# The weighted sum of expert rows moves from VectorE to TensorE

## The reference, cut to what matters

```python
top_s, pos = lax.top_k(combo, PEER_TOPK)
expert = jnp.take_along_axis(ids, pos, axis=-1)
g = jax.nn.softmax(top_s, axis=-1).astype(hb.dtype)
u_sel = peer_u[expert]
a = jax.nn.gelu(jnp.einsum('bqhkd,bqd->bqhk', u_sel, hb))
v_sel = peer_v[expert]
return jnp.einsum('bqhk,bqhkd->bqd', g * a, v_sel)
```

## Time and profile before

| | |
|---|---|
| time, three runs | 2165.31, 2167.11, 2168.97 us; median 2167.11 |
| profiled execution, span | 2165.9 us |
| PE, DVE busy | 1586.9 us (73%), 1510.4 us (70%) |
| gathered rows | 256 x 1 MB = 268.45 MB, by POOL's queue |
| first gather issued, last one issued | 329.8, 1203.6 us |
| last row sum begins | 1233.1 us |

### The profile page before, as it was taken

The page is one execution under the profiler, slowest core; times in us unless marked ns, Lnnn a source line. Parts: engine busy times, 40 slices in busy tenths (PEclk is TensorE's granted clock), DMA queues, the critical chain, the costliest instruction groups (busy, mean ns, idle before and its releaser), DMA issues.

```text
span 2165.9 us, 24713 instructions
## 1 busy us (share of the span) xinstructions
PE 1586.9 (73%) x9616; PEld 1356.3 (63%) x9616; DVE 1510.4 (70%) x2224; ACT 584.5 (27%) x880; POOL 598.4 (28%) x376
## 2 busy tenths in 40 slices
PE   7999999930007999729400176688999999899997
PEld 2975779930006888614200046688898988598997
DVE  2673695799998778598799975867543744666554
ACT  3433420000002220010000134443443344244443
POOL 1542523243333343334344444533000000000000
PEclk9999995555557999959755598899999999999999
DMA  7444459997788999989999415354542554043442
GB/s 311 156 188 184 157 210 381 422 413 287 303 299 309 424 423 422 423 335 404 409 391 396 167 56 210 141 201 158 205 156 78 195 194 157 0 183 138 186 173 100
DMA packets 57567, 538.46 MB, mean 249 GB/s; under 512 B 6384, under 2 KB 6512, under 8 KB 7152
## 3 DMA queue, kind: packets, MB, share of 16 engines
q1 hardware_dynamic: 20592, 268.48, 31.6%
q0 software_dynamic: 36864, 268.45, 31.1%
HBM read 535.86 MB, written 1.05 MB: 248 GB/s over the span
## 4 chain that ended last, share of the span: by engine, by line
PE 48%; DVE 26%; issue 11%; DMA 11%; ACT 2%; POOL 1%; POOLq 0%; DVEq 0%; SPq 0%; ACTq 0%
PE psum L385 48%; DVE arena L1582 10%; DMA arena<-in_experts,idx_stage 9%; DVE ring_r L1224 3%; DMA ring<-in_w_ffn 1%; DVE small L1579 1%; DVE arena L1621 1%; DVE arena L1571 1%; DVE small L1571 1%; DVE rstd L1251 1%; DVE arena_r L1273 1%; DVE arena L1475 1%; DVE small L1473 1%; DVE small L1524 1%; ACT ring_r L904 0%
## 5 line engine op out<-in xcount | busy, mean ns | idle before, releaser
L1224 DVE TENSOR_TENSOR ring_r<-ring,ring_r 128x1024 fp32r<-128x1024 f32 (+1 forms) x240 | 348.8, 1463 | 284.3 <-ACT ring_r L904 283.1
L385 PE MATMUL psum<-small_r,ring_r 128*128 128x256 f32 x2304 | 438.5, 292 | 65.9 <-DVE ring_r L1224 55.7
L385 PEld LDWEIGHTS psum<-small_r,ring_r 128*128 128x128 f32 x2304 | 375.9, 199 | 70.7 <-DVE ring_r L1224 39.8
L853 POOL DMA_INDIRECT arena<-in_experts,idx_stage x256 | 299.7, 1171 | 389.0 <-DVE arena L1582 314.2
L1571 DVE CUSTOM_DVE_ANT_0 arena<-arena 128x1024 f32<-128x1024 f32 x256 | 313.5, 1225 | 105.9 <-DMA arena<-in_experts,idx_stage 97.0
L1582 DVE SCALAR_TENSOR_TENSOR arena<-arena,small 128x1024 f32<-128x1024 f32 x256 | 335.1, 1309 | 9.2
L385 PE MATMUL psum<-h_t_r,ring_r 128*128 128x256 f32 x1152 | 335.7, 291 | 0.0
L385 PE MATMUL psum<-arena_r,ring_r 128*128 128x256 f32 x2208 | 322.2, 280 | 3.0 <-DVE arena_r L1273 3.0
L904 ACT ACTIVATE ring_r<-ring 128x1024 fp32r<-128x1024 f32 (+1 forms) x240 | 247.9, 1041 | 279.3 <-PE psum L385 207.6
L385 PEld LDWEIGHTS psum<-arena_r,ring_r 128*128 128x128 f32 x2208 | 286.5, 190 | 3.5 <-DVE arena_r L1273 3.4
L1126 ACT ACTIVATE small<-small 128x2 f32<-128x2 f32 x128 | 26.0, 203 | 780.0 <-DVE small L1571 779.9
(11 more groups left out here) (222 smaller groups left out, 1843.3 us busy)
## 6 DMA issues: line engine op xcount, KB each, us to landing
ring<-in_w_ffn SPq DMA_DIRECT2D x33, 2048.0 KB, 11.8
ring<-in_w_in SPq DMA_DIRECT2D x31, 2048.0 KB, 10.2
ring<-in_w_ada SPq DMA_DIRECT2D x30, 2048.0 KB, 11.0
ring<-in_w_ffn SPq DMA_DIRECT2D x24, 1408.0 KB, 9.9
ring<-in_w_out SPq DMA_DIRECT2D x4, 2048.0 KB
ring<-in_peer_wq SPq DMA_DIRECT2D x4, 2048.0 KB, 7.8
ring<-in_p_ret SPq DMA_DIRECT2D x4, 2048.0 KB
arena<-in_experts,idx_stage POOLq DMA_INDIRECT x256, 9.5
```

Source lines behind the costliest of these rows:

```text
L385: return nc.tensor.matmul(o, a, b, start=first, stop=last)
L853: nc.gpsimd.indirect_dma_start(rows[slot % GBUF], None, dram["experts"], bass.IndirectOffsetOnAxis(ap=idx_stage[:, slot:slot + 1], axis=0) ...
L1224: nc.vector.tensor_tensor(whole(i, ring_r), whole(i, ring), upper(i).bitcast(F32), ALU.subtract).then_inc(lo_made, 1)
```

## The change

The weights and the additions move to PE. For every slot DVE writes a 128x128 diagonal matrix with gate x activation of each token on the diagonal (`diag_batch`, which takes the place of `sum_batch`). PE multiplies it with the `v` half of the row, in two float32 matmuls of 512 columns, and accumulates a token tile's 128 slots in PSUM banks 6 and 7. PE's second matmul increments `row_free`. At a tile's end ACT copies the two banks to `y_of[t]`. The work that PE had in one piece is cut into steps, and one step goes ahead of every second batch of diagonals; it has 6 banks in turn meanwhile. `diag` is a ring of 8.

```diff
-        weights = small[:, 1456:1472].rearrange("p (b n) -> p b n", b=8)
+        diag = small[:, 1536:2560].rearrange("p (b n) -> p b n", b=GBUF)
...
+            def background():
+                yield from modulation("ada2_", "w_ada_2", range(MOD_CTX), silu_c2, 2)
+                for _ in range(CHOICE_STEPS + 1 - MOD_CTX):
+                    yield
+                squares("ctx1", hid, KD)
+                pe.wait_ge(sem("h_ctx1"), 1)
+                yield from feed_forward("fc", 1, h_t)
+                yield
+                squares("ctx2", hid, KD)
+                pe.wait_ge(sem("h_ctx2"), 1)
+                yield from by_token("kc", "w_in_2", range(2, 4), h_t, "act")
+                yield from by_token("vc", "w_in_2", range(4, 8), h_t, "act")
+
+            cycle[:] = range(BANKS - 2)
+            bg = background()
+            for n in range(NT * SLOTS // BATCH):
+                if n % 2 == 0:
+                    next(bg, None)
+                t, first = divmod(n, SLOTS // BATCH)
+                if first == 0:
+                    for half in range(2):
+                        pe.wait_ge(*tenant[BANKS - 2 + half])
+                for g in range(n * BATCH, (n + 1) * BATCH):
+                    pe.wait_ge(sem("diag"), g + 1)
+                    for half in range(2):
+                        last = mm(psum[:, BANKS - 2 + half, :], diag[:, g % GBUF, :],
+                                  rows[g % GBUF][:, D + half * BANK:D + (half + 1) * BANK],
+                                  g % SLOTS == 0, g % SLOTS == SLOTS - 1)
+                    last.then_inc(sem("row_free"), 1)
...
             for t in range(NT):
-                pe.wait_ge(sem("experts"), t + 1)
+                pe.wait_ge(sem("y_out"), 2 * t + 2)
...
+                act.wait_ge(sem("row_free"), GBUF + SLOTS * (t + 1))
+                for half in range(2):
+                    nc.scalar.activation(y_of[t][:, half * BANK:(half + 1) * BANK], psum[:, BANKS - 2 + half, :],
+                                         ACT.Copy).then_inc(sem("y_out"), 1)
...
-            def sum_batch(n):
+            def diag_batch(n):
                 t, b = divmod(n, per_tile)
                 v.wait_ge(sem("gelus"), n + 1)
-                gate = flat(best[:, t])[:, b * BATCH:(b + 1) * BATCH]
-                step(TT(weights[:, n % 8, :], acts[:, n % 8, :], gate, ALU.mult))
                 for s in range(BATCH):
                     g = n * BATCH + s
-                    STT(y_of[t], rows[g % GBUF][:, D:2 * D], weights[:, n % 8, s:s + 1], y_of[t],
-                        ALU.mult, ALU.add).then_inc(sem("row_free"), 1)
-                    v.wait_ge(sem("row_free"), GBUF + g + 1)
+                    TS(diag[:, g % GBUF, :], ident, acts[:, n % 8, s:s + 1],
+                       flat(best[:, t])[:, b * BATCH + s:b * BATCH + s + 1], ALU.mult, ALU.mult).then_inc(sem("diag"), 1)
```

More of the change, by code:

```diff
@@ L332, in program @@
         row_landed = [sem(f"row_landed{i}") for i in range(GBUF)]
-        groups, index, turn = [], {}, {"act": 0, "dve": 0}
+        groups, index, bank_of = [], {}, {}
+        cycle, at_bank, tenant = list(range(BANKS)), [0], {}
         def phase_end(q):
@@ L356, in begin @@
             def begin(name, who):
-                i = len(groups)
-                if i >= BANKS:
-                    pe.wait_ge(drained[groups[i - BANKS][1]], groups[i - BANKS][2])
+                bank = cycle[at_bank[0] % len(cycle)]
+                at_bank[0] += 1
+                if bank in tenant:
+                    pe.wait_ge(*tenant[bank])
                 count = 1 + sum(g[1] == who for g in groups)
+                index[name] = len(groups)
+                bank_of[name] = bank
                 groups.append((name, who, count))
-                index[name] = i
-                return psum[:, i % BANKS, :]
+                tenant[bank] = (drained[who], count)
+                return psum[:, bank, :]
             def end(ins):
@@ L397, in by_token @@
                         end(last)
-                    release()
+                        if t == NT - 1:
+                            release()
+                        yield
             def squares(tag, sq, kb):
@@ L690, in _ @@
                 ada_turn(i)
[L693 to L700, removed]
+            def background():
+                yield from modulation("ada2_", "w_ada_2", range(MOD_CTX), silu_c2, 2)
+                for _ in range(CHOICE_STEPS + 1 - MOD_CTX):
+                    yield
+                squares("ctx1", hid, KD)
+                pe.wait_ge(sem("h_ctx1"), 1)
+                yield from feed_forward("fc", 1, h_t)
+                yield
+                squares("ctx2", hid, KD)
[18 more added lines that the diff above has]
+                    last.then_inc(sem("row_free"), 1)
+                if n % (SLOTS // BATCH) == SLOTS // BATCH - 1:
+                    for half in range(2):
+                        tenant[BANKS - 2 + half] = (sem("y_out"), 2 * t + half + 1)
+            for _ in bg:
+                pass
+            cycle[:] = range(BANKS)
             for t in range(NT):
-                pe.wait_ge(sem("experts"), t + 1)
+                pe.wait_ge(sem("y_out"), 2 * t + 2)
                 for i in range(2):
@@ L917, in take @@
                 act.wait_ge(group_done, index[name] + 1)
-                return psum[:, index[name] % BANKS, :]
+                return psum[:, bank_of[name], :]
             def drain(ins):
@@ L1162, in _ @@
                 act.wait_ge(group_done, index[f"mx{i}"] + 1)
-                nc.scalar.activation(flat(mixed_hi[:, 2 * i:2 * i + 2, :]), psum[:, index[f"mx{i}"] % BANKS, :],
+                nc.scalar.activation(flat(mixed_hi[:, 2 * i:2 * i + 2, :]), psum[:, bank_of[f"mx{i}"], :],
                                      ACT.Copy).then_inc(sem("mixed_hi"), 1)
@@ L1572, in dot_batch @@
                                                         dots[:, n % 8, s:s + 1]), sem("dots"))
-            def sum_batch(n):
+            def diag_batch(n):
                 t, b = divmod(n, per_tile)
                 v.wait_ge(sem("gelus"), n + 1)
-                gate = flat(best[:, t])[:, b * BATCH:(b + 1) * BATCH]
-                step(TT(weights[:, n % 8, :], acts[:, n % 8, :], gate, ALU.mult))
                 for s in range(BATCH):
                     g = n * BATCH + s
-                    STT(y_of[t], rows[g % GBUF][:, D:2 * D], weights[:, n % 8, s:s + 1], y_of[t],
-                        ALU.mult, ALU.add).then_inc(sem("row_free"), 1)
-                    v.wait_ge(sem("row_free"), GBUF + g + 1)
+                    TS(diag[:, g % GBUF, :], ident, acts[:, n % 8, s:s + 1],
+                       flat(best[:, t])[:, b * BATCH + s:b * BATCH + s + 1], ALU.mult, ALU.mult).then_inc(sem("diag"), 1)
             for t in range(NT):
                 gates(t)
-                step(nc.vector.memset(y_of[t], 0.0))
                 dot_batch(t * per_tile)
@@ L1593, in _ @@
                         dot_batch(n + 1)
-                    sum_batch(n)
+                    diag_batch(n)
                     if b % 2 == 1:
                         next(bg, None)
-                step(nc.vector.memset(stat[:, 0:1], 0.0), sem("experts"))
             for _ in bg:
```

## The result

The changed kernel takes 2300.94 us (median of 4, 2297.22 to 2302.66) against 2166.21 before: ratio 1.0623, 95% interval 1.0608 to 1.0638. The forecast was 2289, with a range of 2228 to 2372. The profiled execution has a span of 2300.8 us, 134.9 more than before. DVE begins to add the expert sums to x at 1366.9 us instead of 1234.5: 132.4 us of the difference lie in the expert layer, where the forecast had put 121.

What follows compares the result with a forecast made beforehand. Before, DMA bound A, C and E, and DVE B and F; after, PE mostly binds. Stretches sum to 1012 us against 891, +121, and +1 for end copies: 2288, median 2289 us, range 2228 to 2372.

Steps and rivals of the forecast that it cites:

- A: Layer stretch from 345 to 502 us before, the modulation; 10 periods of 19.8 us, 198 us forecast, +41.
- C: Layer stretch from 676 to 840 us before, 11 slabs of w13; 249 us forecast including a norm, +85.
- D: Layer stretch from 840 to 978 us before, 8 slabs of w2 and one empty period; 145 us forecast, +7.
- E: Layer stretch from 978 to 1125 us before, 12 steps of keys and values; 187 us forecast including a norm, +40.
- The rival of the collision: DVE's diagonal writes await POOL's gather issues, 4.8 us more per period in B: +56, 2345 us; chance 8 in 100.
- that of the low clock: PE's clock stays low in A and B, +78 and +44: 2411 us; chance 9 in 100.
- B: Layer stretch from 502 to 676 us before, no slab; 12 periods of 10.5 us, 126 us forecast, -48.
- That of the transfers: Transfers bind the layer and PE fits beneath: 785 us for the layer, so 2061 us; chance 4 in 100.
- F: Layer stretch from 1125 to 1236 us before, rows alone; 10 periods of 9.9 us plus 8, 107 us forecast, -4.
- The two norms: Norms of the context, priced in C and E: 17 us each, with 10 to 20 us as ends.
- The semaphore wait of each slot: Each slot's wait might expose a weight load of some 0.19 us: up to +32 us over 42 periods PE binds.
- The write: DVE's diagonal write of 128 columns, taken as 0.28 us, 72 us in all; ends 0.18 or 0.405 us.

Runs made afterwards that it cites:

- half of the matmuls: Changed kernel with the second of the two diagonal matmuls left out for all slots but a tile's first and last: 2186.41 us, ratio 1.0094.
- the tying alone: Kernel before, DVE's row sums kept, PE's list cut into one slab per 4 slots, then a wait for freed rows: 2170.73 us, ratio 1.0012.
- ACT's writes: Changed kernel, but ACT writes the diagonals and DVE only multiplies gate and activation: 2293.61 us, ratio 1.0593.
- mixed kernel: Changed kernel, but PE sums only batches 14 to 43 and 96 to 127, DVE the others; PE's slabs in one piece each: 2139.45 us, ratio 0.9861.
- POOL's wait: POOL's first late addition waits until all rows are freed: 2161.8 us in the kernel before; 2140.11 us when PE sums only batches 14-43 and 96-127.
- the later batch: PE sums batches 14-43 and the second tile from 101 instead of 96, DVE the others, POOL's late additions waiting: 2131.49 us, ratio 0.984.

## Why the prediction came out

**The direction and its cause were right.** The load on PE, 454 us by the sum of the rows, was 473 net (913 - 440). The diagonal matmuls alone make a group of 504 us, 440 at the price of full clock; the rest is their time at the low clock, and part of it is made up by the modulation, which ran partly at full clock. In A, C, D and E the time is a sum of PE's periods; with half of the matmuls 85% of the loss goes away, with the tying alone 4 us come. The rival of the collision is answered by the run with ACT's writes, that of the low clock by a clock of 0.70 in A and 0.88 in B. That of the transfers is answered by the run with half of the matmuls: it takes some 216 us (252 x 0.859) off PE, which leaves some 697 on PE, below the 785 us of that rival's sum, and still the kernel is at 2186 and not near 2061.

**By stretches**, forecast and measured: A 198 and 193; B 126 and 138.5; C 249 and 241.5; D 145 and 145; E 187 and 181.5; F 107 and 121.5. The sum was 1012 and came to 1021. That it is off by 9 only is partly luck: B and F were 27 us too short, A, C and E 18 too long.

- A: I had 9.4 us for 8 diagonals and 10.4 for the slab; it was 10.0 and 11.0, as the clock rose some 5.9 us into the diagonals (I took 4.5) and lasted 3 us into the slab (as taken). The stretch came out shorter all the same: its last two periods took 17.3 us, and the first of the ten slabs, which I had counted in, ran from 319.9 on, ahead of the rows and of the stretch. The 6 us until the first diagonals, at 351.2, go the other way.
- The price of a matmul was taken at 0.888 from keys and values, where some ran at the low clock. At full clock it is 0.859. With slabs of 13.8 and 6.87 us it makes a period of C 20.7 in place of 21.1 and one of E 13.7 in place of 14.2, 5 us in each stretch. The two norms, with the slower slab behind each, took 14 us in place of 17. In E the late cut hides 3 us.
- D met its 145 us by luck: its 8 periods with a slab were 4 us shorter than forecast, and the empty one took 14 us in place of 10, with a wait of 5 for a row.
- The semaphore wait of each slot shows nothing: within 16 records there is no gap. That term, 0 to 32 us, is 0 where PE binds.
- B is a term that was mis-sized: 11.5 us a period, not 10.5. The write took 0.345 us, not 0.28; four of them add 0.26. In the mixed kernel the 30 batches from 14 to 43 took 168 us, 11.2 us a period. From the end of the last slab of modulation to the norm, 13 periods, it is 148 us in the changed kernel, 143 with ACT's writes, and 137 with half of the matmuls. Neither DVE's time nor PE's alone is the bound there, and both have a share in it. That fits the chain that a buffer of the ring goes through (issue, landing, dots, write, PE), but no run changed the ring: argued, not shown.
- My "-48" for B was not a gain of that size. I cut before at 676, behind the context's norm, and priced the norm in C for the changed kernel. Like with like, the norm starts at 656.2 before and at 676.5 after. By that cut B gained 16 us (154.2 to 138.5). The sum over the layer isn't touched, but I carried 35 us into the expectation of the mixed kernel and was wrong there by 12.
- F: 99 us at 9.9 was right in its middle (4.97 us per batch), but two things were missing. The first one is at F's start, the second at its end:

```profile
1234.13 10.46 PE L389 MATMUL psum<-arena,small 128*128 128x512 f32 x24
1258.21 5.78 PE L389 MATMUL psum<-arena,small 128*128 128x512 f32 x8 [13.62 <-DVE small L1621]
...
1299.94 3.70 PE L389 MATMUL psum<-arena,small 128*128 128x512 f32 x8 [1.27 <-DVE small L1621]
1304.90 3.70 PE L389 MATMUL psum<-arena,small 128*128 128x512 f32 x8 [1.26 <-DVE small L1621]
```

When PE's last slab is done, it has to wait 13.6 us for the next rows. Their gathers had just been issued, as PE freed the buffers, and SP issued three loads of 2 MB at the same moment. The DMA engines were full while PE was idle (columns as in the table of the stretches), and the seven gathers from 1236.8 on took 19.2 us at the median to land, 9.1 in the whole run:

```profile
1234.33 0.33 SPq L849 DMA_DIRECT2D ring<-in_w_ada  x1
1234.70 0.43 SPq L849 DMA_DIRECT2D ring<-in_w_ffn  x1
1235.17 0.43 SPq L849 DMA_DIRECT2D ring<-in_w_ada  x1
...
1245.00:1250.00 5.00, 0.00 (x0) 0.00 (x0) 0.95 (x1) 0.00 (x0) 0.98 (x2) 0.88 1.00 424
1250.00:1255.00 5.00, 0.00 (x0) 0.00 (x0) 0.28 (x2) 0.00 (x0) 0.00 (x0) 0.50 1.01 429
```

The next stage's slabs are loaded when PE's list lets go of their ring, and the change moved that moment from E's middle (1052.8 before) to F's start. They are 6.3 MB, 14.8 us at 424 GB/s, a term that F's sum lacked. This is read from the trace; no run moved the slabs. At the end PE's last burst has 12 matmuls and begins at the low clock: from the last dot to DVE's first addition it is 12.4 us, where it was 5.8 before.

## What to carry to other kernels

Before work is moved to an idle engine, add up the busy time of both engines in the stretch in question and compare it with the length of that stretch: here 440 + 454 us in 891 said that PE had no room, though by themselves they would have cost next to nothing. Then do it by periods, since the idle time may lie where the new work can't go, and that is where most of the loss came from; the same change, made only in the two places where PE was idle, made the kernel faster by 1.6% together with two small repairs (POOL's wait and the later batch). When the stretches of two kernels are compared, cut both at the same instruction.

## What the runs showed of the hardware

POOL's copies, and in the mean its issues of gathers, got faster when DVE's row sums were gone. Groups of POOL while gathers are issued, before and after:

```profile
L853 POOL DMA_INDIRECT arena<-in_experts,idx_stage x247 | 291.1, 1179 | 383.3 <-DVE arena L1582 314.2 <-issue 42.5 <-POOL idx_stage L846 26.6
L846 POOL COPY idx_stage<-ids 128x8 uint32 x31 | 37.3, 1203 | 151.9 <-DVE arena L1582 151.9
```
```profile
L889 POOL DMA_INDIRECT arena<-in_experts,idx_stage x248 | 258.9, 1044 | 450.0 <-PE psum L389 389.4 <-issue 39.9 <-POOL idx_stage L882 20.7
L882 POOL COPY idx_stage<-ids 128x8 uint32 x31 | 11.0, 355 | 274.9 <-PE psum L389 274.9
```

A copy of 8 columns takes 0.36 us instead of 1.20. The mixed kernel has both forms in one execution; its copies from 660 to 1010, where DVE sums the rows, and from 1060 to 1170, where PE does:

```profile
L871 POOL COPY idx_stage<-ids 128x8 uint32 x12 | 14.4, 1201 | 53.1 <-DVE arena L1607 53.1
L871 POOL COPY idx_stage<-ids 128x8 uint32 x5 | 1.9, 381 | 9.6 <-PE psum L391 9.6
```

I read it so: where a row sum released the copy, it ran beside the next one, which reads two inputs in SBUF and takes 1.285 us; now a matmul releases it. In the kernel before, too, the first copy, at 326.4 and ahead of any dot, took 0.19 us. That both engines hold each other up fits the rule that the Trainium skill gives (SBUF — State Buffer, section "Who interferes with whom").

With the issues it is less simple. They took 0.94 us at the least in both kernels, but in B they were no faster after the change (1196 ns in the mean) than before (1144), though no row sum is left there. By the same rule the write of the diagonal could collide with them. With ACT's writes the issues of B took 1094 ns, and those of F 1071, where they had been 953. The write itself took 0.345 us at the median. So no run here shows a collision of the writes with the issues, and a difference of a tenth of a microsecond per issue, in either direction, stays unexplained; the collision at the tail, with POOL's additions, is shown.
